# RWKV mixer: the first head pair's factor, values and reads set between its merge products, its inverse ahead of the second Gram, modulation rows turned two chunks later

## The chip, the cores and the metric

The kernel runs on one core of one Trainium2 chip and is written engine by engine: five instruction streams (TensorE = PE, VectorE = DVE, ScalarE = ACT, GpSimd = POOL, SyncE = SP) that meet only at semaphores. The metric is the time of one execution on the device, in microseconds (us); lower is better. 38,816 instructions run in about 2,040 us, so a single one weighs little; what counts is which engine waits for which.

## What is computed

One inference step through two trunk layers with 384 tokens (128 context, 256 latent), width 1024, all in fp32. Each layer runs three token mixers on one normalised input (attention, gated linear attention, RWKV-7), merges them by gates, and ends with an output projection and a SwiGLU block. The change touches the schedule around the RWKV mixer, whose recurrence is, per head and direction:

```python
def rwkv7_scan(r, decay, k, v, a_vec, b_vec, s0):
    def step(s, inp):
        rt, wt, kt, vt, at, bt = inp
        sa = jnp.einsum('bhij,bhj->bhi', s, at)
        s = s * wt[:, :, None, :] + sa[..., None] * bt[:, :, None, :] + vt[..., None] * kt[:, :, None, :]
        return s, jnp.einsum('bhij,bhj->bhi', s, rt)
...
    y_f, sr_f = rwkv7_scan(r, dec_f, kd_f, vc, -kk, kk * a_f, sr_f0)
    y_b, sr_b = rwkv7_scan(flip_t(r), flip_t(dec_b), flip_t(kd_b), flip_t(vc),
                           flip_t(-kk), flip_t(kk * a_b), sr_b0)
    y = y_f + flip_t(y_b)
```

The adaLN modulation, `mod = (silu(cond) @ w_ada + b_ada)`, is computed beside it in pieces, as are the gates `sigmoid(p[..., OFF_GATE:])` and the branch projections `o_a @ w_po_a`, `o_b @ w_po_b`.

## The kernel before

**Phases.** Each layer has five phases, closed by a barrier (L351) at which the compute engines meet. Phase 0 is the input projection, 1 attention, 2 gated linear attention, 3 RWKV, 4 the merge, the output projection and the SwiGLU block. Phase 3 runs at about 404 to 659 us in the first layer and 1403 to 1656 us in the second.

**The RWKV phase.** The 8 heads stand in 4 head pairs, n = 0 to 3; each pair (a "batch" here) holds both directions and 6 chunks of 64 tokens. For each batch the work is a chain of small 64x64 products on PE with evacuations by DVE and ACT between them:

- per half batch (a pair and a direction, g = 0 to 7): `loras` (PE, L862), `decays` and `exps` (ACT, L1575 to L1596), `logs`, `keys`, `terms` (DVE, L2101 to L2137);
- `grams(n)`: the Gram product NG (PE, L883), masked by DVE (L2146 to L2153);
- the inverse of the Gram's 16x16 diagonal blocks: `begin` (DVE, L2159) hands POOL a transposed copy, `off_blocks` (POOL, L1272) and `substitution` (POOL, L1279 to L1286, 28 operations in a chain) work on it, `inverses` (DVE, L2164 to L2173) waits for POOL's result and lays it out;
- `merges(n)`: the products MM, QQ (PE, L990), SS (L999), EE, FF (L990) that grow the 16x16 inverses to 64x64, each waiting for the evacuation of the one before (DVE: QQ L2219, SS L2223, EE L2227, FF L2229; ACT: MM L1626);
- `factor(n, d)` (PE: MT L932, BK L943; DVE L2239, L2243; ACT L1604), `values(n)` (PE L524, L958; ACT L1616), `turned(n)` (PE L969) and `read(n)` (PE L990, ACT L1626): independent of the merges, wanted by what follows them;
- `transitions(n)` (PE: WZ, VZ, RT, FT L990, GG L999; DVE L2188 to L2197), three `scan_step`s (PE L1034, DVE L2208), `outputs(n)` (PE L1047, L1053; ACT L1658).

For n = 1 and 2 the `factor`, `values`, `turned` and `read` of the batch are issued inside `merges(n)`. For n = 0 they stand ahead of the loop, around `grams(1)`; for n = 3 they stand behind `outputs(2)`.

**What fills PE's gaps.** `side_steps` is a generator of independent PE work: gate chunks (L624, 8 matmuls in 4 steps), branch projections "po" (L630, 4 matmuls in 2 steps), modulation chunks "ada" (L621, one step). `fill(k)` takes k steps; the tuple `FILLS` says how many at each place of phase 3. The phase's plan has 48 steps in this order: po, gate for j = 0 to 3, then ada 8 to 11, then po 4, gate 6, po 5, gate 7, po 6, po 7, ada 12 to 15; the number of steps already taken decides which kind stands at a place. Side results go to two PSUM banks in turn, so a side item waits until the one two before it has been emptied by DVE or ACT, and these take up side results only just before their next own wait (`side_work`), in program order.

**Turning the rows.** An ada product lands as a row; ACT copies it to one of two buffers (`modrow`, L1340), and `turn_mod` (PE, L603) turns it to columns, which DVE adds to `mod` (L1801). ACT's copy of a row waits until the row two before it has been turned. Whether a row is turned at once or later is decided here (L639):

```python
                    while len(rows) > (2 if kind == "ada" else 0):
                        turn_mod(*rows.pop(0))
```

SP streams the weights through a ring of three slots; each load waits for the last use of the slot.

## Time and profile before

| | us |
|---|---|
| three runs of the kernel before | 2041.91, 2029.80, 2041.27 (median 2041.27) |
| the profiled execution | 2040.51 |
| its span in the trace | 2038.7 |
| busy in the span: PE / DVE / ACT / POOL | 1826.6 / 1025.7 / 736.7 / 149.4 |
| RWKV phase, layer 0 | 404 to 659 |
| RWKV phase, layer 1 | 1403 to 1656 |

Times of the trace count from the start of the span. A row of the timeline gives start, duration, engine, line, operation, tiles written and read, shape and count, and in brackets how long the engine was idle just before and what released it. In the timeline every fp32 matmul of the program appears as two (x4 is two matmuls of the code). Line numbers are those of the kernel before.

### The profile page before, as it was taken

What the parts mean: (1) busy time and instruction counts of PE and PEld (TensorE: products, weight loads), DVE (VectorE), ACT (ScalarE), POOL (GpSimd) and SP (SyncE); (2) the same over time, 40 slices, a digit from 0 to 9 for tenths busy, and PEclk for the clock granted to TensorE, in tenths of its full rate; (3) what the DMA queues carried; (4) which work ended last, traced back from release to release, by engine and by line L of the source; (5) the groups of instructions that cost most, each with busy time, mean ns of one, the idle gap of its engine ahead of it and who ended that gap; (6) DMA issues with size and microseconds to landing.
All of it is one profiled execution on the core that took longest, in us unless ns stands there. A gap on an engine that the chain in (4) does not pass through costs nothing.

```text
span 2038.7 us, 38816 instructions
## 1 busy us (share of the span) xinstructions
PE 1826.6 (90%) x16819; PEld 1544.8 (76%) x16819; DVE 1025.7 (50%) x1827; ACT 736.7 (36%) x1297; POOL 149.4 (7%) x325
## 2 busy tenths in 40 slices
PE   5899898878796999999989989888687989999998
PEld 2899455546564989999989975555466669899998
DVE  1426438888544453333342444597775345533332
ACT  2334434333233343333243443523332333433321
POOL 2000000034110000000000000000522000000000
PEclk8899999989798999999999999999888989999999
DMA  7443231201304444663443433311012234344342
GB/s 259 166 127 114 89 110 47 81 9 44 105 3 145 145 135 131 185 166 106 128 134 106 126 96 100 111 51 47 2 61 89 84 117 127 94 126 130 112 116 85
DMA packets 267937, 214.48 MB, mean 105 GB/s; under 512 B 7226, under 2 KB 259545, under 8 KB 267513
## 3 DMA queue, kind: packets, MB, share of 16 engines
q1 hardware_dynamic: 264816, 204.41, 33.1%
q0 software_dynamic: 2736, 7.54, 1.2%
q8 instruction: 134, 2.20, 0.5%
q14 instruction: 35, 0.28, 0.0%
q10 hardware_dynamic: 216, 0.06, 0.0%
HBM read 209.10 MB, written 2.88 MB: 104 GB/s over the span
## 4 chain that ended last, share of the span: by engine, by line
PE 72%; DVE 17%; ACT 5%; issue 4%; DMA 1%; SPq 0%; ACTq 0%; POOL 0%; DVEq 0%; POOLq 0%
PE bank L565 12%; PE bank L570 12%; PE bank L566 12%; PE bank L624 8%; PE bank L1188 3%; PE bank L1186 3%; PE bank L1187 3%; PE bank L990 3%; DVE gate L2076 3%; PE bank L621 2%; PE bank L630 2%; PE bank L524 1%; PE bank L999 1%; PE bank L932 1%; PE bank L603 1%
## 5 line engine op out<-in xcount | busy, mean ns | idle before, releaser
L566 PE MATMUL bank<-scr_rounded 128*128 128x384 f32 x1344 | 453.6, 337 | 0.0
L566 PEld LDWEIGHTS bank<-scr_rounded 128*128 128x128 f32 x1344 | 254.9, 190 | 1.3
L565 PE MATMUL bank<-scr_rounded,gate_rounded 128*128 128x384 f32 (+1 forms) x672 | 229.0, 341 | 12.7 <-ACT scr_rounded L1372 9.5
L565 PE MATMUL bank<-scr_rounded 128*128 128x384 f32 (+1 forms) x672 | 227.0, 338 | 9.2 <-ACT scr_rounded L1372 8.7
L624 PE MATMUL bank<-h,ring 128*128 128x384 f32 x576 | 218.8, 522 | 10.9 <-DVEq L351 9.6
L570 PE MATMUL bank<-scr_rounded,gate_rounded 128*128 128x384 f32 (+1 forms) x672 | 223.2, 338 | 0.0
L570 PE MATMUL bank<-scr_rounded 128*128 128x384 f32 (+1 forms) x672 | 221.8, 336 | 0.0
L1816 DVE TENSOR_TENSOR scr_rounded<-ring,gate_rounded 128x2048 fp32r<-128x2048 f32 (+3 forms) x65 | 135.4, 2083 | 159.1 <-ACT gate_rounded L1361 158.4
L1816 DVE TENSOR_TENSOR scr_rounded<-ring,scr_rounded 128x2048 fp32r<-128x2048 f32 (+1 forms) x65 | 135.4, 2083 | 144.3 <-ACT scr_rounded L1361 143.7
L624 PEld LDWEIGHTS bank<-h,ring 128*128 128x128 f32 x576 | 108.7, 200 | 92.1 <-issue 38.0
L1361 ACT ACTIVATE gate_rounded<-ring 128x2048 fp32r<-128x2048 f32 (+3 forms) x65 | 113.6, 1747 | 153.2 <-PE bank L570 67.9
L1361 ACT ACTIVATE scr_rounded<-ring 128x2048 fp32r<-128x2048 f32 (+1 forms) x65 | 113.5, 1746 | 146.9 <-PE bank L570 84.5
L565 PEld LDWEIGHTS bank<-scr_rounded,gate_rounded 128*128 128x128 f32 (+1 forms) x672 | 127.9, 190 | 15.5 <-issue 11.0
L565 PEld LDWEIGHTS bank<-scr_rounded 128*128 128x128 f32 (+1 forms) x672 | 126.9, 189 | 10.9 <-issue 9.3
L570 PEld LDWEIGHTS bank<-scr_rounded,gate_rounded 128*128 128x128 f32 (+1 forms) x672 | 127.3, 190 | 0.5
L570 PEld LDWEIGHTS bank<-scr_rounded 128*128 128x128 f32 (+1 forms) x672 | 126.3, 189 | 0.6
L2380 DVE TENSOR_TENSOR arena<-bank,arena 128x384 f32<-128x384 f32 x44 | 24.5, 558 | 170.5 <-PE bank L570 166.5
L630 PE MATMUL bank<-arena,ring 128*128 128x384 f32 x256 | 97.4, 518 | 6.3 <-DVEq L351 4.1
L621 PE MATMUL bank<-ring,scond 128*2 128x256 f32 x768 | 57.7, 423 | 24.3 <-ACT modrow L1340 13.5
L630 PEld LDWEIGHTS bank<-arena,ring 128*128 128x128 f32 x256 | 47.4, 197 | 37.1 <-issue 12.3
L830 PEld LDWEIGHTS bank<-scr 64*128 64x128 f32 x672 | 42.1, 188 | 36.2 <-DVE scr L2058 21.6
L830 PE MATMUL bank<-scr 64*128 64x128 f32 x672 | 50.6, 287 | 18.5 <-DVE scr L2058 11.0
(386 smaller groups left out, 3180.0 us busy)
## 6 DMA issues: line engine op xcount, KB each, us to landing
ring<-in_w_in_dram SPq DMA_DIRECT2D x56, 1024.0 KB, 5.3
ring<-in_w_ada_dram SPq DMA_DIRECT2D x48, 1024.0 KB, 5.2
ring<-in_w_ffn_in_dram SPq DMA_DIRECT2D x88, 512.0 KB, 5.3
ring<-in_w_ffn_out_dram SPq DMA_DIRECT2D x32, 704.0 KB, 4.6
ring<-in_w_out_dram SPq DMA_DIRECT2D x8, 1024.0 KB, 5.0
ring<-in_w_po_a_dram SPq DMA_DIRECT2D x4, 1024.0 KB, 6.0
ring<-in_w_po_b_dram SPq DMA_DIRECT2D x4, 1024.0 KB, 6.2
ring<-in_w_po_c_dram SPq DMA_DIRECT2D x4, 1024.0 KB, 9.8
```

The lines of the kernel that those rows point to most:

```text
L565: pe.matmul(o, w_hi[:, k, :], right[0][k], start=k == 0, stop=False)
L566: pe.matmul(o, w_lo[:, k, :], right[0][k], start=False, stop=False)
L570: ins = pe.matmul(o, w_hi[:, k, :], right[1][k], start=False, stop=k == nk - 1)
L621: ins = pe.matmul(b[strip:strip + 2, 0:256], scond[:, :, k], w[:, k, :], start=k < 4, stop=k >= 4)
L624: ins = pe.matmul(b[:, 0:T], w[:, k, 128 * (j % 2):128 * (j % 2) + 128], h[:, k, :], start=k == 0, stop=k == KD - 1)
L630: ins = pe.matmul(b[:, 0:T], w[:, k, 128 * (j % 4):128 * (j % 4) + 128], src[:, k, :], start=k == 0, stop=k == 3)
L830: ins = pe.matmul(b[:, CH * cc:CH * cc + CH], zc, zc, start=True, stop=True)
L990: ins = pe.matmul(pair[d][hr[cols(d, h)], 64 * c:64 * c + 64], left(d, h, r, c), right(d, h, r, c), start=True, stop=True)
L1186: pe.matmul(b[:, 0:T], w_hi[:, k, :], ff_hi[n], start=n == 0, stop=False)
L1187: pe.matmul(b[:, 0:T], w_hi[:, k, :], ff_lo[n], start=False, stop=False)
L1361: A(shaped(whi[m % 2], name, j), weights(l, name, j), ACT.Copy).then_inc(*tells("w_hi"))
L1816: tt(shaped(wlo[m % 2], name, j), weights(l, name, j), value(shaped(whi[m % 2], name, j)), sub).then_inc(*tells("w_lo"))
```

## The change

Three things are done, in both layers:

1. `factor(0, 0)`, `factor(0, 1)`, `values(0)`, `turned(0)`, `read(0)` leave their places around `grams(1)` on PE, ACT and DVE and are issued inside `merges(0)`, as those of batches 1 and 2 already are. Three `fill`s inside `merges(0)` and two around the old places go with it.
2. On DVE `inverses(0)` comes before `grams(1)` (and before the moved `factor`), and `begin(1)` no longer stands inside `inverses(0)` but behind `grams(1)`. `begin(2)` and `begin(3)` stay where they were in effect.
3. `turn_mod` is always held back until two more rows have come, whatever kind of side work is running; what is left is turned at the end of the phase.

`FILLS` becomes 29 numbers that sum to 46 instead of 34 that sum to 48 (two more steps are taken elsewhere in the phase by a plain `fill(2)`): the side work is 2 steps behind before's from `transitions(0)` on, and the 48 steps are just used up by the last `fill`.

```diff
-        FILLS = (4, 4, 0, 2, 1, 1, 1, 0, 1, 1, 1, 2, 1, 1, 1, 1, 2, 2, 2, 1, 1, 2, 2, 2, 1, 1, 1, 2, 1, 1, 1, 2, 1, 1)
+        FILLS = (4, 4, 0, 2, 2, 2, 2, 1, 1, 1, 1, 2, 2, 2, 1, 1, 2, 2, 2, 1, 1, 1, 2, 1, 1, 1, 2, 1, 1)
...
-                    while len(rows) > (2 if kind == "ada" else 0):
+                    while len(rows) > 2:
                         turn_mod(*rows.pop(0))
...
-                    if n in (1, 2):
+                    if n < 3:
                         factor(n, 0)
                     else:
                         fill(next(steps))
...
                 loras(3)
                 fill(next(steps))
-                factor(0, 0)
-                factor(0, 1)
-                values(0)
-                fill(next(steps))
                 grams(1)
                 loras(4)
-                fill(next(steps))
-                turned(0)
-                read(0)
                 fill(next(steps))
...
                     dve.transpose(Zc.rearrange("p u j -> p j u"), W.rearrange("p j a i -> p j (a i)")).then_inc(*tells("rw_zc"))
                     dve.wait_ge(*last())
-                    if n < 3:
-                        begin(n + 1)
...
-                factor(0, 0)
-                factor(0, 1)
+                inverses(0)
                 grams(1)
+                begin(1)
                 logs(4)
-                inverses(0)
                 for n in range(4):
...
                     if n < 3:
                         inverses(n + 1)
+                    if n < 2:
+                        begin(n + 2)
```

**PE, from the factor of batch 0 to its first merge products.** Each row is a line of the kernel, the tiles and the count. Before (the factor of the first direction, L932 and L943, stands just ahead of the first row):

```order
L932 MATMUL bank<-scr 64x128 x24
L943 MATMUL bank<-cst,scr 64x64 x24
L524 MATMUL bank<-cst,arena 128x128 x3
L958 MATMUL bank<-cst,arena 64x128 x6
L624 MATMUL bank<-h,ring 128x384 x2
L883 MATMUL bank<-scr 64x64 x24
L862 MATMUL bank<-arena,lora 128x384 x2
L630 MATMUL bank<-arena,ring 128x384 x2
L969 MATMUL bank<-cst,scr 64x64 x24
L990 MATMUL bank<-arena,gate 64x64 x24
L990 MATMUL bank<-arena,scr 64x64 x24
L990 MATMUL bank<-scr,arena 64x64 x24
```

The same place of the change, from the second Gram (L883) on; MM and QQ are the two rows of L990:

```order
L883 MATMUL bank<-scr 64x64 x24
L862 MATMUL bank<-arena,lora 128x384 x2
L630 MATMUL bank<-arena,ring 128x384 x4
L990 MATMUL bank<-arena,scr 64x64 x24
L990 MATMUL bank<-scr,arena 64x64 x24
L932 MATMUL bank<-scr 64x128 x24
L943 MATMUL bank<-cst,scr 64x64 x24
L999 MATMUL bank<-scr,cst 64x64 x24
L932 MATMUL bank<-scr 64x128 x24
L943 MATMUL bank<-cst,scr 64x64 x24
```

The Gram now follows the half batches' terms directly, and the two factor halves stand behind QQ and behind SS (L999).

**DVE, the same place.** Before: the factor's masks (L2239, L2243), the Gram's (L2146 to L2153), `logs(4)` (L2101 to L2105), `inverses(0)` (L2164 to L2173), `begin(1)` (L2159).

```order
L2239 TENSOR_TENSOR gate<-bank,cst 128x384 x8
L2243 TENSOR_SCALAR scr<-scr,small 128x64 x2
L2146 TENSOR_TENSOR cst<-bank,cst 128x384 x2
L2151 SCALAR_TENSOR_TENSOR lora<-cst 128x384
L2153 SCALAR_TENSOR_TENSOR cst<-lora,cst 128x12x16
L2101 SCALAR_TENSOR_TENSOR scr<-cst,arena 128x384
L2103 TENSOR_TENSOR scr<-scr 128x384
L2105 TENSOR_TENSOR scr<-scr,arena 128x384
L2164 STREAM_TRANSPOSE scr<-cst 128x16x32
L2169 TENSOR_TENSOR scr<-scr,cst 128x384 x2
L2173 STREAM_TRANSPOSE scr<-cst 128x16x32
L2159 STREAM_TRANSPOSE cst<-cst 128x512
```

In the change the line numbers of these statements are 12 lower; the last two rows are the evacuation of a po chunk (L1808 and L1810 before).

```order
L2152 STREAM_TRANSPOSE scr<-cst 128x16x32
L2157 TENSOR_TENSOR scr<-scr,cst 128x384 x2
L2161 STREAM_TRANSPOSE scr<-cst 128x16x32
L2134 TENSOR_TENSOR cst<-bank,cst 128x384 x2
L2139 SCALAR_TENSOR_TENSOR lora<-cst 128x384
L2141 SCALAR_TENSOR_TENSOR cst<-lora,cst 128x12x16
L2147 STREAM_TRANSPOSE cst<-cst 128x512
L2089 SCALAR_TENSOR_TENSOR scr<-cst,arena 128x384
L2091 TENSOR_TENSOR scr<-scr 128x384
L2093 TENSOR_TENSOR scr<-scr,arena 128x384
L1796 SCALAR_TENSOR_TENSOR gtmp<-gtmp,bank 128x384
L1798 TENSOR_TENSOR mg<-mg,gtmp 128x384
```

The inverse has gone ahead of the Gram, the factor's masks are gone from here, and a po chunk is taken up ahead of QQ's evacuation.

**PE, from the scan of batch 1 to the first product of batch 2.** L1034 is the scan, L1047 and L1053 `outputs(1)`, L883 `grams(3)`, L621 an ada chunk, L603 a row turned. Before:

```order
L621 MATMUL bank<-ring,scond 2x256 x16
L1034 MATMUL bank<-scr 64x64 x4
L621 MATMUL bank<-ring,scond 2x256 x8
L603 MATMUL bank<-cst,modrow 128x2 x2
L621 MATMUL bank<-ring,scond 2x256 x8
L603 MATMUL bank<-cst,modrow 128x2 x2
L1047 MATMUL bank<-gate,arena 64x64 x24
L1053 MATMUL bank<-scr 64x64 x20
L630 MATMUL bank<-arena,ring 128x384 x2
L883 MATMUL bank<-scr 64x64 x24
L630 MATMUL bank<-arena,ring 128x384 x2
L603 MATMUL bank<-cst,modrow 128x2 x4
```

And in the change:

```order
L624 MATMUL bank<-h,ring 128x384 x4
L1034 MATMUL bank<-scr 64x64 x4
L621 MATMUL bank<-ring,scond 2x256 x16
L1047 MATMUL bank<-gate,arena 64x64 x24
L1053 MATMUL bank<-scr 64x64 x20
L621 MATMUL bank<-ring,scond 2x256 x8
L603 MATMUL bank<-cst,modrow 128x2 x2
L883 MATMUL bank<-scr 64x64 x24
L621 MATMUL bank<-ring,scond 2x256 x8
L603 MATMUL bank<-cst,modrow 128x2 x2
```

All ada chunks stand two steps later, and no pair of rows is turned behind `grams(3)`.

## Rows read from the trace of the kernel before

**Rows 1.** The page, part 4: chain that ended last, by engine.
```profile
PE 72%; DVE 17%; ACT 5%; issue 4%; DMA 1%; SPq 0%; ACTq 0%; POOL 0%; DVEq 0%; POOLq 0%
```

**Rows 2.** Window, RWKV phase, layer 0: length; PE, PEld, DVE, ACT, POOL busy; clock; DMA.
```profile
404.00:659.00 255.00, 202.80 (x4201) 146.49 (x4202) 155.68 (x319) 85.82 (x201) 60.56 (x136) 0.90 0.20 64
```

**Rows 3.** Timeline of PE, layer 0, up to the merges of batch 0.
```profile
445.44 2.84 PE L932 MATMUL bank<-scr 64*64 64x128 f32 x48 [8.00 <-DVE gate L2239]
...
460.91 0.93 PE L990 MATMUL bank<-arena,scr 64*64 64x64 f32 x48 [2.61 <-DVE scr L2169]
```

**Rows 4.** Timeline of DVE, same stretch.
```profile
443.60 0.64 DVE L2137 TENSOR_TENSOR scr<-arena,scr 128x384 f32<-128x384 f32 x1
...
453.15 1.02 DVE L2146 TENSOR_TENSOR cst<-bank,cst 128x384 f32<-128x384 f32 x2 [3.48 <-PE bank L883]
...
455.45 0.96 DVE L2101 TENSOR_TENSOR_SCAN scr<-cst,arena 128x384 f32<-128x384 f32 x1
456.45 1.66 DVE L2103 TENSOR_TENSOR scr<-scr 128x384 f32<-128x384 f32 x1
...
458.73 1.06 DVE L2164 STREAM_TRANSPOSE scr<-cst 128x512 f32<-128x512 f32 x1
...
461.86 0.71 DVE L2159 STREAM_TRANSPOSE cst<-cst 128x512 f32<-128x512 f32 x1
462.61 1.02 DVE L2219 TENSOR_TENSOR scr<-bank,cst 128x384 f32<-128x384 f32 x2
...
474.50 1.02 DVE L2188 TENSOR_TENSOR scr<-bank,scr 128x384 f32<-128x384 f32 x2 [3.15 <-PE bank L990]
```

**Rows 5.** Timeline of POOL: last operations of the first substitution, then `off_blocks(1)`.
```profile
444.77 0.24 POOL L1286 TENSOR_TENSOR cst<-cst,lora 128x28 f32<-128x28 f32 x1
455.50 2.19 POOL L1272 TENSOR_TENSOR cst<-cst 128x768 f32<-128x768 f32 x1 [10.49 <-DVE cst L2153]
```

**Rows 6.** Windows as in Rows 2, where PE restarts.
```profile
444.00:448.00 4.00, 2.56 (x48) 2.59 (x52) 3.13 (x7) 0.00 (x0) 0.85 (x3) 0.50 0.00 0
448.00:452.00 4.00, 4.00 (x75) 2.94 (x67) 1.42 (x5) 2.38 (x8) 0.00 (x0) 0.85 0.01 4
```

**Rows 7.** Timeline of DVE, batches 1 and 2: QQ (L2219) and RT (L2188) evacuated.
```profile
500.38 1.02 DVE L2219 TENSOR_TENSOR scr<-bank,cst 128x384 f32<-128x384 f32 x2
...
517.77 1.02 DVE L2188 TENSOR_TENSOR scr<-bank,scr 128x384 f32<-128x384 f32 x2 [7.06 <-PE bank L990]
...
555.41 1.02 DVE L2219 TENSOR_TENSOR scr<-bank,cst 128x384 f32<-128x384 f32 x2 [2.64 <-PE bank L990]
...
571.75 1.02 DVE L2188 TENSOR_TENSOR scr<-bank,scr 128x384 f32<-128x384 f32 x2 [5.12 <-PE bank L990]
```

**Rows 8.** Timeline of PE, scan of batch 1 to merges of batch 2.
```profile
521.52 2.85 PE L624 MATMUL bank<-h,ring 128*128 128x384 f32 x8
...
531.44 1.89 PE L621 MATMUL bank<-ring,scond 128*2 128x256 f32 x16 [2.38 <-ACT modrow L1340]
...
543.61 0.93 PE L883 MATMUL bank<-scr 64*64 64x64 f32 x48
...
551.59 0.98 PE L603 MATMUL bank<-cst,modrow 128*128 128x2 f32 x4 [5.22 <-DVE gtmp L1808]
552.50 1.56 PE L990 MATMUL bank<-arena,scr 64*64 64x64 f32 x48
```

**Rows 9.** Timeline of DVE, same stretch.
```profile
534.08 0.55 DVE L2137 TENSOR_TENSOR scr<-arena,scr 128x384 f32<-128x384 f32 x1
...
544.60 1.02 DVE L2146 TENSOR_TENSOR cst<-bank,cst 128x384 f32<-128x384 f32 x2 [6.73 <-PE bank L883]
```

**Rows 10.** Timeline of PE, merges of batch 3, layer 0 and layer 1.
```profile
623.30 1.89 PE L621 MATMUL bank<-ring,scond 128*2 128x256 f32 x16 [1.91 <-DMA ring<-in_w_ada_dram]
...
1623.41 1.89 PE L621 MATMUL bank<-ring,scond 128*2 128x256 f32 x16 [3.12 <-DMA ring<-in_w_ada_dram]
```

**Rows 11.** Timeline of DVE at the end of phase 2, layer 0.
```profile
404.44 0.15 DVE L1801 TENSOR_TENSOR mod<-bank,par 128x4 f32<-128x4 f32 x1
```

More of the change, by code:

```diff
@@ L899, in merges @@
                         chunkwise("SS", "V", n, d, lambda h, c: Mm[hr[h], d, c, :], lambda h, c: Am[hr[h], d, c, :])
-                    if n in (1, 2):
+                    if n < 3:
                         factor(n, 1)
@@ L906, in merges @@
                     crossed("EE", "V", n, lambda d, h: h, lambda d, h: h ^ d, lambda d, h, r, c: Mm[r, d, c, :], lambda d, h, r, c: Sm[d][r, c, :])
-                    if n in (1, 2):
+                    if n < 3:
                         values(n)
@@ L914, in merges @@
                     crossed("FF", "V", n, lambda d, h: h ^ d, lambda d, h: h, lambda d, h, r, c: (Sm[0], Zn[1])[d][r, c, :], lambda d, h, r, c: (Zn[0], Sm[1])[d][r, c, :])
-                    if n in (1, 2):
+                    if n < 3:
                         turned(n)
-                    if n in (1, 2):
+                    if n < 3:
                         read(n)
@@ L1663, in merges @@
                         copied("MM", Mm, n, d)
-                    if n in (1, 2):
+                    if n < 3:
                         factor(n, 0)
@@ L1697, in _ @@
                 exps(3)
-                factor(0, 0)
-                factor(0, 1)
-                values(0)
                 decays(4)
-                turned(0)
-                read(0)
                 for n in range(4):
@@ L2219, in merges @@
                         tt(Am[:, d, :, :], taken("QQ", n, d), over(K("eye"), 6), add).then_inc(*empties("QQ", l, n, d))
-                    if n in (1, 2):
+                    if n < 3:
                         factor(n, 0)
@@ L2223, in merges @@
                         tt(Sm[d], taken("SS", n, d), over(K("eye"), 6), add).then_inc(*empties("SS", l, n, d))
-                    if n in (1, 2):
+                    if n < 3:
                         factor(n, 1)
@@ L2290, in _ @@
                     terms(g)
-                factor(0, 0)
-                factor(0, 1)
+                inverses(0)
                 grams(1)
+                begin(1)
                 logs(4)
-                inverses(0)
                 for n in range(4):
```

## The prediction

> **What bounds the kernel now.** I read the chain that ended last first: PE holds 72% of it, DVE 17% [rows 1]. Most of that is dense projection work that the change leaves alone. The change lies in the RWKV phase, so I read that phase by itself, from the window, then the timelines of PE, DVE and POOL. PE is busy 202.8 of 255 us there [rows 2], with the granted clock at 0.90; 52 us per layer are gaps, and only gaps and low clock can be won. The reader should find two kinds. The first is starvation ahead of the first batch: PE sits idle 8.00 us until DVE empties a bank of the factor, then 2.61 us until DVE has laid out the inverse [rows 3]. The second is between batches 1 and 2: PE waits 2.38 us for ACT's copy of a modulation row and 5.22 us for DVE to empty a side bank before it may turn a row [rows 8], while DVE itself idled 6.73 us waiting for the Gram NG(3), which PE reached at 543.61 although its input was ready at 534.6 [rows 8, 9]. Each waits for the other in turn; that ring is what the late row turning cuts.
>
> **The sum, per layer.** I use layer 0's times; layer 1 repeats them. A gain counts only where the chain passes it on.
>
> *A. First batch earlier.* The marker is DVE's evacuation of QQ, at 462.6 before [rows 4]. In the change DVE ends its terms at 444.2 [rows 4] and wants the inverse, but POOL's last operation ends at 445.0 [rows 5]: that is the new floor. From there, all on DVE: the inverse 3.1 (458.73 to 461.86), the Gram's masks 2.3 (453.15 to 455.45), `begin(1)` 0.7, `logs(4)` 3.3 (455.45 to 458.73), all [rows 4], then the po chunk that now stands ahead of QQ, two operations like L2137's 0.64, less their overlap, 1.1. 445.0 + 3.1 + 2.3 + 0.7 + 3.3 + 1.1 = 455.5, 7.1 earlier. PE is not later than that: it restarts at 444.4 on a clock of 0.50 and is at 0.85 over the window after [rows 6], so the Gram (1.5), the loras (3) and the po fill (3) end near 452 and MM and QQ (1.8) near 454, the durations being those of such pieces at the one clock or the other. The price is inside the batch. From QQ's to RT's evacuation the first batch took 474.50 - 462.61 = 11.9 [rows 4]; batches 1 and 2, which carry their factor inside, took 17.4 and 16.3 [rows 7]. I take their mean, 16.8, so 4.9 is given back, and 0.3 more as batch 1's scan starts a little later behind RT than batch 0's did. A = 7.1 - 4.9 - 0.3 = 1.9. The bounds: 5.5 given back and a slow start (454 becomes 457 if PE's clock stays low) make -1; nothing given back makes +7. The far ends are kept for the range.
>
> DVE and POOL slow each other here, which is why `logs(4)` costs 3.3: its middle operation took 1.66 us under `off_blocks(1)`, while `off_blocks(1)` took 2.19 beside it, against 0.64 and 0.55 for other operations of its shape [rows 4, 5, 9]. After the move the same two stand side by side again, so I kept the slow price. The Trainium skill, SBUF — State Buffer, section "Who interferes with whom", says that a DVE instruction with two SBUF inputs and a GpSimd instruction that reads SBUF exclude each other for a whole instruction. By that rule it depends on who comes first: if POOL does, DVE waits up to a whole `off_blocks`, 2.2 instead of the 1.1 lost in the row, and A would be 0.8; if DVE does, it loses nothing and A would be 3.0. The stretched 1.66 agrees with the rule.
>
> *B. A po chunk moves in front of QQ(1)*, where DVE has no gap (its row at 500.38 shows no wait [rows 7]): -1.1.
>
> *C. Batch 1 to batch 2.* The scan's second-last fill is now 8 gate matmuls, 2.85 us, where two ada chunks stood, about 1.9 (1.89 for half of them at half clock) [rows 8]: 0.9 later, so the last scan step is at 529.5 instead of 528.6 and DVE's terms end at 535.4. Then PE: ada 8 at once; ada 9 when ACT has emptied the gate's bank behind its exponentials, near 531.5; `outputs(1)` (3.0 at full clock), ada 10, one turn (0.5): the Gram starts at 537.0 and DVE has it at 537.9 instead of 544.60, 6.7 earlier. What follows on DVE takes 4.7 (the Gram 2.3, the inverse up to what PE wants of it 2.4 of the 3.1 [rows 4], in a stretch with POOL at work), so PE may go on at 542.6. Before, PE reached MM(2) only at 552.50, since it stood 5.22 us at the turn [rows 8]; now the last turn is done by 539.5, so MM(2) starts at 542.6: 9.9 earlier. If the half us gap before ada 9 is enough to bring PE to its lower clock, as after the 2.38 us gap (1.89 us for 16 matmuls), `outputs(1)` and the rest take 3.1 longer and C is 6.8. I take 9.0.
>
> *D. A po chunk now ends right before the first scan step of batch 2*, DVE takes it up first: -0.7.
>
> *E. Batch 3.* Before, an ada load kept PE waiting 1.91 and 3.12 us inside the merges [rows 10]; po fills stand there now, whose weights are already in: +2.8 on the mean of both layers (the replaced fills are about as long). But ada chunks and their turns now stand between the scan steps and before `outputs(3)`: -1.9. E = +0.9, between -2 and +3.
>
> *F. Phase ends.* Two rows left over are turned together at the end of phases 1 and 2. In phase 2 the last turn needs the bank that DVE empties only at its last instruction, at 404.44 [rows 11], so PE turns and DVE adds once more behind it: -0.9. In phase 1 one more turn stands before the last head's product: -0.9.
>
> Sum per layer: 1.9 - 1.1 + 9.0 - 0.7 + 0.9 - 1.8 = 8.2; two layers 16.4. The long PE-bound stretch after batch 2 passes the gain on, since its amount of work is the same. Against the profiled execution of 2040.5 us that makes 2024. The median of the runs shown, 2041.27, is 0.8 above the profiled one, which changes nothing. The runs themselves spread from 2029.8 to 2041.9.
>
> **The rivals.**
>
> *R1, the row turning pays, and the first batch pays in full.* If the 4.9 given back in A isn't, because MT and BK products fill gaps of DVE's that batches 1 and 2 don't have, A is 7 and with C at 9.9 the layer 14.2: 2040.5 - 28.4 = 2012. For it: PE has 4 us of slack at the new start. Against it: both rows of batches with this order show 16 to 17 us [rows 7].
>
> *R2, the waits come back.* PE's wait for a row's copy or for a side bank moves from `grams(3)` to the outputs or the scan, since ACT copies rows only between its other work and DVE empties banks only at its own next wait. Then C is only the wait that ended just before MM(2), 552.50 less the 549.3 at which the inverse was ready (544.60 + 4.7), 3.2; the layer has 2.4: 2036. For it: the two banks are unchanged. Against it: the walk in C shows each bank empty but for half a us.
>
> *R3, slower.* The stretch between the last fill and the Gram is now wholly idle on PE (the factor's first half stood there), from about 433 to 444, and the batch behind it consists of nothing but 64x64 products with waits between them. If PE stays at the lower of its clocks (0.50 [rows 6]) through the whole merge of batch 0, its 12 us of work there takes twice as long; 12 more, less the 2 in which it was waiting anyway, A = -8. With the rest at +6.3 the layer loses 1.7 and the kernel stands at 2044. It decides from A = -6.3 on, that is when more than about two thirds of the batch runs at half clock. Against it: in the window after the restart the clock was back at 0.85 [rows 6], behind an idle time of 8.00.
>
> R4, no effect beyond 2 us: the ring of waits was not on the chain. Against it is DVE's idle 6.73, released by the Gram itself [rows 9].
>
> **How the numbers follow.** Forecast 0.52, R1 0.20, R2 0.17, R3 0.07, R4 0.04. The likeliest case gives 2024. Its own range is 2016 (A at +4, C at 9.9, E at +2: 12.3 per layer) to 2032 (A at 0, C at 6.8: 4.1). The range reaches to R1 and R2: 2008 to 2036. About 1% is what a measurement of this kernel can tell from no change, 20.4 us, so the border is 2021. Faster by over 1%: all of R1 and two fifths of the forecast case, 0.41. Within 1%: the rest of the forecast case, R2, R4 and most of R3, 0.54. Slower by over 1%: 0.05, an R3 that also meets low clock in C.
>
> **What the profile of the changed kernel would show.** A: QQ of batch 0 evacuated near 455.5, RT near 472.3 (before 474.5); an RT under 469 speaks for R1, over 476 for R3, whose mark is a clock of 0.5 between 450 and 465. C: no turn between `grams(3)` and MM(2), NG(3) evacuated some 7 us sooner after the last scan step than before, no wait of PE for gtmp over 1 us; a wait over 2 us before `outputs(1)` or MM(2) would be R2. B and D: L1808 directly in front of QQ(1) and of the first scan step of batch 2. E: no DMA wait in the merges of batch 3, waits of PE for modrow between its scan steps. F: two more additions to `mod` at DVE's end of phase 2, the barrier 1 us later. The forecast is wrong if a phase outside RWKV moves by over 2 us, or if the two layers differ by more than 5.

## The result, and the profile after

The changed kernel takes 2029.97 us (median of 20 runs, 2019.77 to 2036.12), the kernel before 2041.97 us (median of 20 runs beside them). The ratio is 0.9942, with a 95% interval of 0.9931 to 0.9952: 11.8 us faster, between 9.8 and 14.1. The forecast was 16.4 us. The profiled execution spans 2027.4 us, where that of before spans 2038.7: 11.3 us less. The chain has moved little, from DVE to PE:

```profile
PE 73%; DVE 16%; ACT 4%; issue 4%; POOL 2%; DMA 1%; SPq 0%; ACTq 0%; DVEq 0%; POOLq 0%
```

The window of the RWKV phase of layer 0 (length, then busy PE, PEld, DVE, ACT, POOL, clock, DMA) is 8 us shorter, with PE busy 2.5 us less, as [rows 2] has it for before:

```profile
404.00:651.00 247.00, 200.33 (x4205) 144.05 (x4206) 154.93 (x318) 85.84 (x201) 59.78 (x136) 0.89 0.21 65
```

Line numbers on DVE are lower by 14 from the merges on (QQ is evacuated at L2205, RT at L2174), those on ACT and POOL by 7, and those on DVE up to L2161 by 12. First the timeline of PE up to batch 0, which answers [rows 3]:

```profile
444.44 1.56 PE L883 MATMUL bank<-scr 64*64 64x64 f32 x48 [13.31 <-DVE scr L2125]
445.93 2.92 PE L862 MATMUL bank<-arena,lora 64*128 64x384 f32 x4
448.78 4.24 PE L630 MATMUL bank<-arena,ring 128*128 128x384 f32 x8
452.95 0.93 PE L990 MATMUL bank<-arena,scr 64*64 64x64 f32 x48
```

PE is now idle 13.31 us in one piece. Then its Gram, loras and po fill run at a clock of 0.50 (window 444 to 448) and 0.55 (448 to 452), and MM starts at 452.95. DVE, against [rows 4]:

```profile
445.26 1.07 DVE L2152 STREAM_TRANSPOSE scr<-cst 128x512 f32<-128x512 f32 x1 [0.88 <-POOL cst L1279]
...
448.37 1.02 DVE L2134 TENSOR_TENSOR cst<-bank,cst 128x384 f32<-128x384 f32 x2
...
451.31 1.70 DVE L2089 TENSOR_TENSOR_SCAN scr<-cst,arena 128x384 f32<-128x384 f32 x1
453.05 1.00 DVE L2091 TENSOR_TENSOR scr<-scr 128x384 f32<-128x384 f32 x1
...
455.73 1.01 DVE L2205 TENSOR_TENSOR scr<-bank,cst 128x384 f32<-128x384 f32 x2
...
472.63 1.02 DVE L2174 TENSOR_TENSOR scr<-bank,scr 128x384 f32<-128x384 f32 x2 [6.88 <-PE bank L990]
```

Between batches 1 and 2 PE's waits of [rows 8] are gone, and so is its low clock there (0.50 from 532 to 540 before, 1.00 now; it falls only behind that, to 0.55 from 540 to 544, where PE waits for DVE's inverse):

```profile
530.25 1.04 PE L621 MATMUL bank<-ring,scond 128*2 128x256 f32 x16 [0.58 <-ACT gtmp L1346]
...
537.09 0.45 PE L883 MATMUL bank<-scr 64*64 64x64 f32 x13 [0.70 <-issue]
537.99 1.05 PE L621 MATMUL bank<-ring,scond 128*2 128x256 f32 x16 [0.45 <-DMA ring<-in_w_ada_dram]
538.97 0.61 PE L603 MATMUL bank<-cst,modrow 128*128 128x2 f32 x4
542.35 1.56 PE L990 MATMUL bank<-arena,scr 64*64 64x64 f32 x48 [2.78 <-DVE scr L2157]
```

In batch 3 something has come instead. Timeline of PE behind RT(3), then three windows of 4 us (the last three numbers are clock, DMA share, GB/s):

```profile
618.48 0.74 PE L990 MATMUL bank<-arena,scr 64*64 64x64 f32 x34
622.92 0.70 PE L990 MATMUL bank<-arena,scr 64*64 64x64 f32 x14 [3.69 <-issue]
623.55 2.83 PE L999 MATMUL bank<-arena 128*64 128x64 f32 x48
626.30 1.89 PE L621 MATMUL bank<-ring,scond 128*2 128x256 f32 x16
628.12 1.01 PE L603 MATMUL bank<-cst,modrow 128*128 128x2 f32 x4
629.70 1.89 PE L621 MATMUL bank<-ring,scond 128*2 128x256 f32 x16 [0.56 <-ACT modrow L1333]
...
637.28 1.04 PE L621 MATMUL bank<-ring,scond 128*2 128x256 f32 x16 [0.19 <-ACT modrow L1333]
```
```profile
616.00:620.00 4.00, 2.90 (x178) 2.66 (x174) 1.02 (x2) 2.58 (x6) 0.00 (x0) 1.00 1.09 364
...
624.00:628.00 4.00, 4.00 (x62) 2.60 (x58) 1.80 (x4) 0.00 (x0) 0.00 (x0) 0.50 0.01 4
...
632.00:636.00 4.00, 4.00 (x43) 2.37 (x43) 1.59 (x7) 0.38 (x1) 0.00 (x0) 0.51 0.96 295
```

PE stands 3.69 us in the middle of a product and waits for nothing that the profile names; this is what its label "issue" means. Behind that the clock is 0.50 until about 636, and the ada chunks and turns, which now stand here, take 1.89 and 1.01 us instead of 1.05 and 0.61. In layer 1 the same wait is 3.42 us; before, it was 3.08 us in layer 0, and in layer 1 there was none at this place.

**The sum laid beside the trace.** Each marker is taken from DVE's start of the phase, and a gain is what it came earlier than before, less what the marker ahead of it did. The columns are forecast, layer 0, layer 1:

| Step (marker at its end) | forecast | layer 0 | layer 1 |
|---|---|---|---|
| A (last scan step of batch 0) | +1.9 | +1.4 | +3.8 |
| B (QQ(1)) | -1.1 | -1.1 | -1.1 |
| C (QQ(2)) | +9.0 | +10.5 | +9.4 |
| D (last scan step of batch 2) | -0.7 | -0.1 | -2.6 |
| from there to QQ(3) | 0 | -0.2 | -0.1 |
| E (last scan step of batch 3) | +0.9 | -2.5 | -2.4 |
| end of the phase | 0 | +0.7 | -0.4 |
| F (phase ends) | -1.8 | -0.6 | -2.7 |
| sum | +8.2 | +8.0 | +3.9 |

That is 11.9 for both layers (the rows are rounded); the rest of the program gives 0.6 back, which makes the 11.3 of the spans. The F of layer 1 holds everything between the two RWKV phases. From barrier to barrier on DVE, the RWKV phase is 8.5 us shorter in layer 0 and 6.8 in layer 1, and no other phase moved by more than 1.5, so neither of the two signs for a wrong forecast came.

### The profile page after: what moved, and what is told of

Read it like the earlier page. It is cut to its first block, busy times and chain, and to the rows that moved or that the text cites. A ratio compares the mean times of both kernels' runs of the same rounds, so it can differ in the third digit from the quotient of the medians.

```text
span 2027.4 us, 38818 instructions
## 1 busy us (share of the span) xinstructions
PE 1822.0 (90%) x16819; PEld 1538.5 (76%) x16819; DVE 1025.8 (51%) x1827; ACT 736.7 (36%) x1297; POOL 148.1 (7%) x325
## 4 chain that ended last, share of the span: by engine, by line
PE 73%; DVE 16%; ACT 4%; issue 4%; POOL 2%; DMA 1%; SPq 0%; ACTq 0%; DVEq 0%; POOLq 0%
PE bank L565 12%; PE bank L570 12%; PE bank L566 12%; PE bank L624 7%; PE bank L1180 3%; PE bank L1181 3%; PE bank L1179 3%; PE bank L990 3%; DVE gate L2064 3%; PE bank L630 2%; PE bank L621 2%; PE bank L524 1%; PE bank L999 1%; PE bank L603 1%; PE bank L932 1%
## 5 line engine op out<-in xcount | busy, mean ns | idle before, releaser
L624 PE MATMUL bank<-h,ring 128*128 128x384 f32 x576 | 211.1, 511 | 11.7 <-DVEq L351 8.3
L565 PEld LDWEIGHTS bank<-scr_rounded 128*128 128x128 f32 (+1 forms) x672 | 127.1, 189 | 10.9 <-issue 9.3
L630 PE MATMUL bank<-arena,ring 128*128 128x384 f32 x256 | 101.8, 537 | 0.7 <-DVEq L351 0.7
L630 PEld LDWEIGHTS bank<-arena,ring 128*128 128x128 f32 x256 | 49.0, 205 | 35.0 <-issue 11.9
L621 PE MATMUL bank<-ring,scond 128*2 128x256 f32 x768 | 58.1, 428 | 16.3 <-ACT modrow L1333 8.0
```

The costliest lines, as they stand in the source:

```text
L565: pe.matmul(o, w_hi[:, k, :], right[0][k], start=k == 0, stop=False)
L621: ins = pe.matmul(b[strip:strip + 2, 0:256], scond[:, :, k], w[:, k, :], start=k < 4, stop=k >= 4)
L624: ins = pe.matmul(b[:, 0:T], w[:, k, 128 * (j % 2):128 * (j % 2) + 128], h[:, k, :], start=k == 0, stop=k == KD - 1)
L630: ins = pe.matmul(b[:, 0:T], w[:, k, 128 * (j % 4):128 * (j % 4) + 128], src[:, k, :], start=k == 0, stop=k == 3)
```

## Experiments

Every ratio is against the kernel before, run on the same chip beside it; us are that ratio times 2041, with the 95% interval. "E5" is the kernel e5, the changed one with the old rule for rows in phases 1 and 2; the kernels e6 to e13 are built on it, but for e8, and e11 has the old rule everywhere.

| Kernel | ratio | us against before |
|---|---|---|
| changed | 0.9942 | -11.8 (-14.1 to -9.8) |
| e1 rows only | 1.0012 | +2.4 (-1.2 to +6.1) |
| e2 changed, old rule for rows | 0.9928 | -14.7 (-18.6 to -10.8) |
| e3 changed, old places | 0.9969 | -6.3 (-9.4 to -3.3) |
| e5 changed, old rule in phases 1 and 2 | 0.9923 | -15.7 (-20.0 to -11.4) |
| e6 E5, last ada chunks at the end | 0.9980 | -4.1 (-8.2 to -0.2) |
| e7 E5, logs behind the merges | 0.9917 | -16.9 (-22.0 to -12.0) |
| e8 places only | 0.9955 | -9.2 (-11.8 to -6.3) |
| e9 E5, factor ahead of batch 0 | 0.9922 | -15.9 (-20.2 to -11.8) |
| e10 E5, weight loads early | 0.9931 | -14.1 (-19.4 to -9.0) |
| e11 e7 and e10, old rule | 0.9921 | -16.1 (-22.0 to -10.4) |
| e12 E5, 3 MB more in batch 3 | 1.0002 | +0.4 (-4.7 to +5.7) |
| e13 E5, 3 MB more in batch 2 | 0.9966 | -6.9 (-12.4 to -1.2) |

**Rows or places?** The prediction gave the 9 us of C to the late turning of rows. Four kernels take the change apart.

e1, the kernel before with one line of the change:

```diff
-                    while len(rows) > (2 if kind == "ada" else 0):
+                    while len(rows) > 2:
```

> The kernel before with the late row turning alone (no row is turned while two or fewer are open), nothing else. Theory T, the rows cut the ring between batches 1 and 2: PE's waits there for ACT's copy of a row (2.38 us) and for the side bank (5.22 us) are gone, batch 2's QQ is evacuated 5 to 8 us earlier per layer, phase ends cost 1.0 to 1.8 back, so 8 to 12 us faster than the kernel before (about 2031). Rival P, the new places of the side work make batch 2 early and the rows only go along: batch 2's QQ moves under 2 us, the phase ends cost the same, and the kernel is 0 to 3 us slower than before.

e2, the changed kernel with that line put back:

```diff
-                    while len(rows) > 2:
+                    while len(rows) > (2 if kind == "ada" else 0):
```

> The changed kernel with the old rule for rows (a row is turned behind the next chunk that isn't ada). Theory T: PE waits again for a bank or a row ahead of MM of batch 2, whose QQ is evacuated 4 to 7 us later than in the changed kernel, phase ends are about 1 us shorter each, so 4 to 10 us slower than the changed kernel, 2 to 8 faster than the kernel before. Rival P (the places do it): within 2 us of the changed kernel, or faster by the 3 us of the phase ends.

e3, the changed kernel with later side work back at the places of before:

```diff
-        FILLS = (4, 4, 0, 2, 2, 2, 2, 1, ...
+        FILLS = (4, 4, 0, 2, 4, 2, 2, 1, ...
```

> The changed kernel with two more side steps where PE stands idle 13.3 us ahead of the first merge, so that all later side work comes two steps earlier: the last four ada chunks stand in the merges of batch 3 and behind them, none between its scan steps. Theory T, what was mis-sized is the ada work between the scan steps of batch 3 at half clock: the last scan step comes 3 to 5 us earlier after FT(3) than in the changed kernel (16.0 us from FT to the last H there, 10 to 12 here), a wait of 1 to 3 us for an ada load comes back in the merges, and the kernel is 3 to 6 us faster than the changed one. Rival: the loads are now so late that the waits in the merges take all of it: within 1.5 us of the changed kernel or slower.

e8, the kernel before with nothing changed but the places:

```diff
-        FILLS = (4, 4, 0, 2, 1, 1, 1, 0, 1, 1, 1, 2, ...
+        FILLS = (4, 4, 0, 2, 1, 1, 1, 0, 1, 0, 0, 2, ...
```

> The kernel before with two fills fewer in the merges of the first batch, so that all later side work comes two steps later, at the places of the changed kernel; the rule for rows, the first batch and the inverse are those of before. Theory P, the places alone make batches 2 and 3 early: QQ(2) 8 to 10 us earlier against QQ(1) per layer, the 2.38 us wait for a row's copy and the 5.22 us wait for a bank both gone, and the kernel 12 to 18 us faster than before. Rival, the first batch and the rows have a share in it: QQ(2) gains under 5 us against QQ(1), the kernel is 0 to 6 us faster.

The rows alone give nothing (+2.4), and without them the change is as good or better (-14.7). The places alone give 9.2 of the 11.8, less than the 12 to 18 expected of them; what e2 has beyond e8, 5.5 with an error of about 5, is the first batch's share. How much earlier QQ(2) comes against QQ(1), in layers 0 and 1: 10.5 and 9.4 us in the changed kernel, 11.0 and 9.1 in e2, 7.9 and 9.4 in e8, but 4.4 and 6.7 in e1 and 4.6 and 4.9 in e3. So the rows do remove a wait, the 5.22 us of [rows 8], and bring about half of C by themselves. But the other wait stays: in e1 and e3 two ada chunks stand together where a gate chunk stands now, and a third then waits for ACT's copy of the first row. In e1's trace the 11.1 us of C over both layers don't reach the end either: phases 1 and 2 are 8.8 us longer than in before's trace, and the stretch from QQ(3) to the last scan step is 4.7 longer, most of it in layer 1, where PE now stands 3.30 us on issue. Timeline of PE in e3:

```profile
531.27 1.89 PE L621 MATMUL bank<-ring,scond 128*2 128x256 f32 x16 [2.38 <-ACT modrow L1333]
533.09 1.01 PE L603 MATMUL bank<-cst,modrow 128*128 128x2 f32 x4
534.66 1.89 PE L621 MATMUL bank<-ring,scond 128*2 128x256 f32 x16 [0.56 <-ACT modrow L1333]
536.48 1.01 PE L603 MATMUL bank<-cst,modrow 128*128 128x2 f32 x4
537.42 2.83 PE L1047 MATMUL bank<-gate,arena 128*64 128x64 f32 x48
```

What follows the 2.38 us, up to L1047, runs at the lower clock (L1047 takes 2.83, in the changed kernel 1.62). In e8, with the old rule and the first batch of before, both waits are gone; PE waits only for its own issue and for DVE's inverse:

```profile
536.12 1.62 PE L1047 MATMUL bank<-gate,arena 128*64 128x64 f32 x48
...
544.18 0.45 PE L883 MATMUL bank<-scr 64*64 64x64 f32 x13 [2.90 <-issue]
...
549.44 1.56 PE L990 MATMUL bank<-arena,scr 64*64 64x64 f32 x48 [2.89 <-DVE scr L2169]
```

In e2 the old rule meets no po chunk between the Gram and MM(2), so there is no turn that could wait for DVE's bank, and PE waits 1.79 us for DVE's inverse, which is what should end last there:

```profile
540.50 0.61 PE L603 MATMUL bank<-cst,modrow 128*128 128x2 f32 x4
542.90 1.56 PE L990 MATMUL bank<-arena,scr 64*64 64x64 f32 x48 [1.79 <-DVE scr L2157]
```

e3 was meant for the ada work of batch 3 and expected to gain; it lost 5.5, and in its trace that is C, which falls with the places by 5.8 and 4.5 us.

**Phase ends.** e5 keeps the late turning in the RWKV phase alone:

```diff
-            def side_steps(plan):
+            def side_steps(plan, late=False):
...
-                    while len(rows) > 2:
+                    while len(rows) > (2 if kind == "ada" or late else 0):
...
-                side[0] = side_steps(side_plan(l, 3))
+                side[0] = side_steps(side_plan(l, 3), True)
```

> The changed kernel with the late row turning in the RWKV phase alone; phases 1 and 2 turn their rows by the old rule. Theory T: the barrier behind phase 2 is 1 us earlier per layer and phase 1's end 0.5 to 1, so 3 us faster than the changed kernel (2 to 4), the RWKV phase itself unchanged. Rival: the turns at the phase ends are covered by DVE's end, less than 1 us difference.

It is 3.9 us faster than the changed kernel by the ratios, as F's 3.6 wants, though the intervals overlap. A single profile can't show it: phase 1 of layer 0 takes 91.3 to 93.3 us in the eleven kernels with the old rule there. The means of all traces can. Over the three kernels with the late rule (changed, e1, e3), phases 1 and 2 of both layers take 3.6 us more in sum than over those eleven, with an error of about 1.3. At DVE's end of phase 2 the late rule shows in e1, an idle 1.10 that neither before [rows 11] nor e5 has:

```profile
407.92 0.23 DVE L1801 TENSOR_TENSOR mod<-bank,par 128x4 f32<-128x4 f32 x2
409.24 0.16 DVE L1801 TENSOR_TENSOR mod<-bank,par 128x4 f32<-128x4 f32 x1 [1.10 <-PE bank L603]
```

**The first batch.** e9 puts the first batch's factor, values and reads ahead of the merges again, on PE, ACT and DVE; on DVE:

```diff
+                factor(0, 0)
                 inverses(0)
+                factor(0, 1)
                 grams(1)
                 begin(1)
```

> The changed kernel with the old rule for rows in phases 1 and 2, and with the first batch's factor, values and reads ahead of the merges as in the kernel before, DVE's order being half the factor, the inverse, the other half, the Gram. It prices what the batch gives back. Theory T: from QQ(0) to RT(0) takes 12 us instead of 16 to 17, QQ(0) is 2.5 to 3.5 us later than in the changed kernel (near 459), so RT(0) is 1 to 2 us earlier, 2 to 4 us faster in all. Rival: QQ(0) is later by 5 us or more, because the turned products stand ahead of it on PE as well: RT(0) the same or later, 0 to 3 us slower.

e7 takes `logs` out of DVE's path to QQ:

```diff
                 begin(1)
-                logs(4)
                 for n in range(4):
-                    if n == 1:
-                        logs(6)
                     merges(n)
+                    if n < 2:
+                        logs(2 * n + 4)
```

> The changed kernel with the old rule for rows in phases 1 and 2, and on DVE logs(4) and logs(6) behind the merges of batches 0 and 1 instead of ahead of them. It prices logs in the path to QQ: theory T, QQ(0) is evacuated 3.3 us earlier (near 451), the logs fall into the 6 us that DVE idles ahead of RT, and RT(0) and RT(1) come 2 to 3 us earlier, so 4 to 8 us faster in all than without this. Rival: PE isn't ready, since its products for QQ come after the loras at low clock; QQ(0) moves by under 1.5 us and ACT's exponentials for batch 2 come late, which delays terms(4) by 2 us or more: no gain or slower.

In e9 QQ(0) to RT(0) takes 12.4 and 10.4 us (layers 0 and 1) where E5 takes 17.2 and 14.8, but QQ(0) is later by 6.0 and 5.3, and RT(0) by 1.2 and 0.8. The total is that of E5. This is the rival's case. So what the batch gives back is the factor's own work, wherever it stands, and its new place is worth nothing by itself. With the factor where before has it, e9 still ends batch 0's scan 1.7 and 4.5 us earlier than before, where e8, which drops the same two fills but leaves the inverse behind the Gram, gains at most 0.7. What is left between the two is the inverse ahead of the Gram, `begin(1)` with it, and one more fill gone from `merges(0)`; the inverse is the likely one, but no run moves it alone. In e7 DVE has 3.3 us less to do ahead of QQ(0), but then waits 2.29 us for PE's po chunk and 0.45 for QQ itself, and QQ(0) is where E5 has it, within 0.4:

```profile
455.85 0.55 DVE L1796 SCALAR_TENSOR_TENSOR gtmp<-gtmp,bank 128x384 f32<-128x384 f32 x1 [2.29 <-PE bank L630]
...
457.44 1.02 DVE L2205 TENSOR_TENSOR scr<-bank,cst 128x384 f32<-128x384 f32 x2 [0.45 <-PE bank L990]
```

PE, at half clock behind its long idle time, is as late as DVE. The rival was right on that; QQ(1), where PE isn't late, comes 1.2 and 0.9 earlier, and the total of 1.2 is inside the error.

**The ada work of batch 3.** e6 moves all of it to the phase's end:

```diff
-        FILLS = (... 2, 1, 1, 1, 2, 1, 1)
+        FILLS = (... 2, 1, 1, 1, 0, 0, 0)
```

> The changed kernel with the old rule for rows in phases 1 and 2, and no side work behind batch 3's transitions, between its scan steps or ahead of its outputs: the last four ada chunks and their turns all stand at the phase's end, behind the variance of the last head. Theory T, the ada work among the scan steps is what was mis-sized: from FT(3) to the last H takes 6 to 8 us instead of 15 to 17, the clock stays low for less, and about half comes back at the end, where PE now has 7 us of work in a gap of 4: 3 to 7 us faster than the kernel with the old rule in phases 1 and 2 alone. Rival: the four slots of the ring come free late, the loads of the next phase are late by 3 us or more and its start waits for them: no gain, or slower by up to 6.

From DVE's evacuation of FT(3) to its first normalisation behind the scan it takes 6.0 and 5.7 us in layers 0 and 1, in before 8.9 and 8.8, in E5 10.7 and 9.8, in the changed kernel 13.8 and 10.9. So this work costs 4 to 5 us in E5, and 5 to 8 in the changed kernel. It comes back at the end, with interest: each chunk now waits for ACT's copy of the row ahead of it, and the clock is at 0.50 again. PE starts the next phase 6.7 us later than in E5 (layer 0, from the start of the RWKV phase), and the kernel is 11.6 us slower than E5. The rival had the sign right and the cause wrong (it named the loads).

**PE standing on issue.** Three kernels ask why PE stands 3 to 4 us in RT and FT of batch 3. e10 does the last po chunks before the merges, so that the loads which they release are over by then:

```diff
-        FILLS = (... 1, 1, 1, 2, 1, 1, 1, 2, 1, 1)
+        FILLS = (... 1, 1, 1, 5, 1, 1, 0, 1, 1, 0)
```

> The changed kernel with the old rule for rows in phases 1 and 2, and three more side steps behind the variances of batch 2, so that the last po chunks are done ahead of batch 3's merges and the weight loads which they release run then, not beside RT and FT of batch 3; two ada chunks stand in the merges, one behind the transitions and one between the scan steps. Theory S, PE stands 3.4 to 4 us on issue at RT/FT of batch 3 because its program is fetched over the same DMA engines as the weight loads (350 GB/s then): the wait shrinks to 1 to 1.9 us as in batches 0 to 2, the clock doesn't fall to 0.50 behind it for longer than 4 us, and from FF(3) to the last H takes 3 to 5 us less: 4 to 8 us faster than the kernel with the old rule in phases 1 and 2 alone. Rival: the wait is the program's own at this place and stays at 3 us or more; gain under 2 us, from one ada chunk fewer among the scan steps.

e12 adds three transfers to SyncE's queue; e13 puts the same lines ahead of the queue's wait for a ring slot (in both, POOL also waits for them at the layer's end, which isn't shown). A line of PE is one higher in these two:

```diff
+                if (name, j) == ("ada", 21):
+                    sp.wait_ge(*emptied("FF", l, 2, 0))
+                    for i in range(3):
+                        sp.dma_start(scratch[l, i], source(l, "ada", i)).then_inc(extra, 16)
```

> The changed kernel with the old rule for rows in phases 1 and 2, and with three added transfers of 1 MB each per layer from device memory to device memory, which nothing uses, put on the weight loads' queue when the FF product of batch 2 has been emptied, a stretch in which the DMA engines are silent. Theory S: PE's waits on issue in RT and FT of batch 2, 1.08 and 1.74 us in layer 0 without the transfers, become 3 us or more in one of them, and the granted clock falls behind it. Rival: they stay at 0.7 to 1.8 us, and the long wait of batch 3 has another cause.

> The same three added transfers of 1 MB per layer as in the run before, which went out only beside the weight loads of batch 3, because the queue waits for a ring slot first; here they stand ahead of that wait, so that they go out when the FF product of batch 2 has been emptied, where the DMA engines are otherwise silent. Nothing uses their data. Theory S (PE's waits on issue are its program's fetch, stretched by whatever else is on the DMA engines): in RT or FT of batch 2 one of the waits, 1.08 and 1.74 us in layer 0 and 1.11 us in layer 1 without the transfers, becomes 3 us or more, as in batch 3, and the granted clock falls behind it. Rival: both stay under 2 us, and the long wait of batch 3 has another cause.

In e12 the transfers didn't go out in batch 2, since the queue waited for its slot first; they ran beside the loads of batch 3. PE's wait there was 4.52 and 3.97 us, against 3.97 and 3.51 in E5. That shows nothing: in the kernels without added transfers and with the loads at this place it lies between 3.1 and 4.7. In e13 they ran where meant, and the waits of batch 2 went from 1.74 us (layer 0) and 1.11 us (layer 1) to 4.21 and 4.40. In the twelve other kernels these two waits lie between 0.9 and 1.8 (the one of layer 1 is missing in before), so this rise is clear. Timeline of PE in E5 and in e13, with e13's windows:

```profile
565.74 0.46 PE L990 MATMUL bank<-arena,scr 64*64 64x64 f32 x14 [1.74 <-issue]
```
```profile
571.11 0.70 PE L991 MATMUL bank<-arena,scr 64*64 64x64 f32 x14 [4.21 <-issue]
571.73 2.83 PE L1000 MATMUL bank<-arena 128*64 128x64 f32 x48
```
```profile
564.00:568.00 4.00, 2.14 (x126) 2.01 (x127) 1.02 (x2) 2.13 (x5) 0.00 (x0) 1.00 1.07 355
568.00:572.00 4.00, 0.89 (x18) 0.77 (x19) 0.15 (x1) 0.00 (x0) 0.00 (x0) 0.66 0.97 304
572.00:576.00 4.00, 4.00 (x51) 3.28 (x50) 1.99 (x4) 0.00 (x0) 0.00 (x0) 0.50 0.08 26
```

e10 is the counterpart. The wait in batch 3 is 0.53 us in layer 0, 1.38 in layer 1, and the clock is 1.00 from 628 on:

```profile
616.24 1.05 PE L621 MATMUL bank<-ring,scond 128*2 128x256 f32 x16 [2.08 <-DMA ring<-in_w_ada_dram]
...
626.54 0.34 PE L990 MATMUL bank<-gate,scr 64*64 64x64 f32 x7 [0.53 <-issue]
```

FF(3) to the last scan step takes 12.9 and 13.8 us, in E5 19.7 and 18.4. Both signs of theory S in the trace hold, its 4 to 8 us do not. Still e10 isn't faster than E5: QQ(3) comes 4.2 us later in layer 0, as three more side steps stand ahead of it, and PE waits 2.08 us for an ada load inside the merges (the first row). In layer 1 it is 9.7 later, of which 5.6 were already lost at QQ(2), in code that both kernels share: there PE stood 2.15 us on issue in RT(0), against 1.88 in E5, and 2.54 in the Gram of batch 3, beside ada loads, where E5 shows no such wait over 0.6 (e8's 2.90 in the Gram of layer 0 is a second one of this kind). Profiles of one execution differ by that much. The totals of e12 and e13 don't price the wait, since the added transfers also push back the weight loads: in e12 PE waits 1.43 and 2.54 us for an ada load between the scan steps, in E5 not at all.

e11 adds the old rule and the late `logs` to e10 ("the first kernel" in its expectation is e10):

> The first kernel of this call with two things more: the old rule for rows in the RWKV phase as well, and logs(4) and logs(6) behind the merges. It is the sum of what the runs so far speak for. Theory: 1 to 2 us more than the first kernel of this call gains, 2015 to 2020 us, 20 us or more faster than the kernel before. Rival: with the old rule a turn stands again ahead of work that DVE or ACT holds up, and it is no faster than the first kernel of this call.

It lands with E5, e7 and e9, 15.7 to 16.9 us under before. These four can't be told apart; all are 4 to 5 us under the changed kernel.

## Why the prediction was right, and where it wasn't

**The way and the range** held: 2030 lies between 2008 and 2036, and within 1% was the likeliest of the three. That layer 0 adds up to 8.0 for 8.2 is luck in part: C, D, F and the phase's end came out 4.0 better than forecast, A and E 3.9 worse.

**A** was right. QQ(0) was expected at 455.5 and evacuated at 455.73; RT at 472.3, found at 472.63; QQ to RT 16.8, found 16.9. That is layer 0. In layer 1, which the prediction took for a repetition, QQ to RT takes 15.5, so less is given back. Over the eight kernels with this first batch, A is 1.2 in layer 0 and 3.0 in layer 1 on the mean, against 1.9 forecast. The price of `logs(4)`, 3.3 beside POOL, was met (451.31 to 454.64). The Trainium skill's rule (SBUF — State Buffer, "Who interferes with whom") lets DVE and POOL exclude each other, and the one that issues first goes first. The rows agree with it:

```profile
450.72 1.48 POOL L1265 TENSOR_TENSOR cst<-cst 128x768 f32<-128x768 f32 x1 [5.56 <-DVE cst L2141]
452.15 1.48 POOL L1291 TENSOR_TENSOR scr<-scr,cst 128x384 f32<-128x384 f32 x1
```

POOL's first operation started ahead of DVE's scan (451.31) and kept the 1.48 us that it has elsewhere. The scan ended 0.81 us behind it, having taken 1.70 instead of 0.96. POOL's second operation ended 0.62 behind the scan, having taken 1.48 instead of 0.83, and DVE's next ended 0.42 behind that, having taken 1.00 instead of 0.56. So DVE lost 1.2 in two pieces. The prediction's 2.2 for the case in which POOL comes first was too much for two reasons: only 0.9 of POOL's operation was left when the scan started, and the 2.19 of before had itself been stretched, from the 1.48 to 1.52 of the other operations of that shape. R3's low clock came for 8 us and ended before the merges.

**B** was right to a tenth. **D** lost 0.1 and 2.6 for 0.7 forecast.

**C had the right size and the wrong cause.** The step that failed is "that ring is what the late row turning cuts". The walk through C was close in its times: the second ada chunk at 530.25 against 531.5, the Gram at 535.60 against 537.0, its evacuation at 537.59 against 537.9, MM(2) at 542.35 against 542.6. Some luck is in the last two, since a wait on issue of 0.70 us inside the Gram took back half of the lead. But it was a walk through the new places as well as the new rule, and I put its whole gain down to the rule. e8 and e2 give it to the places: a gate chunk instead of two ada chunks ahead of the third, and no po chunk between the Gram and MM(2). The rule alone gets about half (4.4 and 6.7), the places all of it without the rule. About 4.2 of the 10 us in layer 0 are clock: ahead of the Gram, two ada chunks took 1.89 us for 1.05, two turns 1.02 for 0.61, L1047 2.83 for 1.62 and L1053 1.82 for 1.38. Two of the signs named for C were wrong in themselves. "No turn between `grams(3)` and MM(2)" contradicts the order of the change, which has one there (538.97). And PE does wait over 2 us before MM(2), 2.78, which was to speak for R2; but what releases it is DVE's inverse, as the walk had it.

**E is the term that was mis-sized**: +0.9 forecast, -2.5 and -2.4 found, outside its own bound of -2; 6.7 us over both layers, more than the 4.6 by which the forecast missed. How much of that is one execution's chance can be seen in E5, whose RWKV phase is the same code: +0.2 and -1.3. Its first half, no load waited for in the merges, was right (QQ(3) to FF(3) 2.3 and 3.5 shorter, for 2.8). Its second half, the ada chunks among the scan steps, was priced at 1.9 from full-clock rows. In E5, where the clock recovers at about 631 in layer 0, it costs 1.9 and 1.0; in the changed kernel, where it stays at 0.50 until 636, 4.9 and 2.0. And layer 1 meets a wait on issue of 3.42 us where before had none. I had read the 3.08 us of before's layer 0 as nothing that the change could touch.

**F** was right in sum, 3.3 for 3.6. e5 and the means over all traces agree with it. That single profiles can't settle it is shown by the start of the RWKV phase in layer 0, which lies between 404.9 and 408.6 us in kernels that share all code up to there.

**The late turning of rows costs** 2.4 us alone (e1) and 2.9 on top of the rest (e2 against the changed kernel). Neither is proved by itself, as the intervals overlap, but both agree with F and with the two turns more that stand among the last scan steps.

R1 fell with A's 1.4 and 3.8, where it wanted 7, and e9 says why: what the batch gives back is its own work. R2 fell with the rows of C, R3 with the clock, and R4 with the result. A slip in the chances: to reach 0.54, the case "within 1%" holds only 0.02 of R3's 0.07, though it says "most of R3", and R3's 2044 lies within 1%.

## What to carry to other kernels

When a change moves work and alters a rule at once, walk through the critical stretch twice, once with each of them undone: a walk with both gives the size, never the cause. A side chunk's price is its duration at the clock that the wait ahead of it leaves, so price it at half clock wherever a gap of over 2 us stands before it, as the mean clock was behind all the waits on issue of 2.3 us or more seen here (a chunk can still be lucky: behind 2.38 us in e1 it took 1.06). And where an engine runs hundreds of very short instructions, keep bulk loads away from that stretch.

## What the runs showed of the hardware

PE's program comes over the same DMA engines as the data. The profile lists a queue of its own for it, with 2.20 MB in 134 packets over the whole program, about 65 bytes for each of PE's 33,638 matmuls and weight loads. Each answer below is the part on DMA queues (packets, MB, share of 16 engines): of the changed kernel at 560 to 563, around a quiet wait (561.40 to 562.59), of the same kernel at 620 to 622, in the long wait (619.23 to 622.92), and of e13 at 567 to 571.2, in its long wait:

```profile
q8 instruction: 1, 0.02, 2.0%
```
```profile
q1 hardware_dynamic: 300, 0.29, 47.2%
q8 instruction: 1, 0.02, 3.6%
```
```profile
q1 hardware_dynamic: 1370, 1.38, 103.6%
q8 instruction: 1, 0.02, 1.4%
```

Worked out from these rows the one packet of the instruction queue keeps one engine busy for about 1 us each time (0.020 x 16 x 3 = 0.96, 0.036 x 16 x 2 = 1.15, 0.014 x 16 x 4.2 = 0.94), loaded or not. What differs is when it starts. By the packed trace, the packet of the quiet wait starts at 560.38, 1.0 us before PE stops, and lands at 561.34; PE goes on 1.25 us later. The packet of the long wait starts at 620.46, 1.2 us after PE has stopped, and lands at 621.62; PE goes on 1.30 us later. The other traces say the same. They hold 220 waits on issue of 0.6 us or more, all in the RWKV phases. Of these, 219 end 1.2 to 1.6 us after such a packet has landed. The same 219 stand at one place of a block of 256 records of PE (matmuls, weight loads and its sequencer's), give or take two, so that two waits of a trace are 256 instructions or a multiple of that apart.

The waits without bulk transfers beside them go up to 2.2 us. With the weight loads or the added transfers beside RT and FT they are 3.1 to 4.7, while the load queue takes 300 to 360 GB/s. These waits hit products of 64x64, where 48 matmuls of the timeline take 0.9 us. The Trainium skill (Runtime: NRT & Kernel Launch, "Instruction fetch mechanics") says that the program is streamed in blocks of 16 KiB, 256 instructions, over a DMA queue and that this is mostly hidden. The blocks agree with the 0.02 MB and with the distance of the waits; here the cost wasn't hidden, and e13 and e10 show it to grow and shrink with the other traffic. So a wait of this kind is PE's wait for its next block. That the block comes late because it queues behind the data is the reading that all rows agree with; no run here moved the fetch by itself, and traffic alone doesn't fix the length: in the Grams beside ada loads the wait is under 0.9 us in most kernels, 2.90 in e8 and 2.54 in e10.

The second surprise is what such a wait does to the clock. Over all traces, in the 4 us behind each of the 28 waits on issue of 2.3 us or more, the mean granted clock was 0.50 to 0.68. Behind the 192 shorter ones it was 0.95 or more but for eight, among them 0.69 behind 1.76 us in layer 1 of before and 0.57 behind 1.59 us in e13. How long the low clock lasts isn't settled by the wait: in layer 0 it was 5 us in E5 and 13 us in the changed kernel, in the same code. That difference is left unexplained.
